# Small SBUF buffers moved to the front, every large buffer at a multiple of 2048 bytes, in a two-layer encoder trunk on one core

## What is computed

```python
x = x + 0.5 * swiglu(rms_norm(x, g1), w_gate, w_up, w_down)      # width 2816
h = rms_norm(x, g2)
xr, yr, q, k, v, g_a, g_b = split(h @ w_in)
y_a = (gelu(yr) * rg_lru(conv(xr))) @ w_up_a                     # recurrence, width 1408
y_b = chunked_attention(norm(q), norm(k), v, rel_table) @ w_up_b # 16 heads of 64
x = x + (sigmoid(g_a) * y_a + sigmoid(g_b) * y_b) @ w_out
x = x + 0.5 * swiglu(rms_norm(x, g3), w_gate2, w_up2, w_down2)
```

## Time and profile before

| | |
|---|---|
| median of 3 runs | 2804.24 us (2801.92 to 2804.95) |
| span of the profiled execution | 2802.1 us |
| mean granted clock of TensorE | 0.995 |
| PE busy | 2759.9 us, 98% of the span |
| POOL, ACT, DVE busy | 42%, 42%, 30% |
| DMA queue of the weights | 28.8% of 16 engines |

### The profile page before, as it was taken

One profiled execution on the slowest core, in us unless ns is written; L12 is line 12 of the kernel. 1 busy time (PEld: TensorE's weight loads), 2 busy tenths in 40 slices (PEclk: granted clock), 3 DMA queues, 4 the chain that ended last, 5 costly groups with the idle time before them and its releaser, 6 DMA issues.

```text
span 2802.1 us, 35532 instructions
## 1 busy us (share of the span) xinstructions
PE 2759.9 (98%) x11968; PEld 2198.7 (78%) x11968; DVE 831.6 (30%) x1515; ACT 1187.7 (42%) x1680; POOL 1179.1 (42%) x524
## 2 busy tenths in 40 slices
PE   8999999999999999999999999999999999999998
PEld 6888878878776688888888888788787757888887
DVE  4222035630015432221142211448100164322222
ACT  5443235742445534443244432457324463444422
POOL 3444444444442234444444444344453422444444
PEclk9999999999999999999999999999999999999999
DMA  7323223332331223232233223232333212223222
GB/s 257 98 92 99 94 84 96 91 100 82 98 98 40 71 91 101 94 99 95 93 99 97 90 94 98 82 94 83 109 94 98 72 41 89 91 90 105 94 91 87
DMA packets 247056, 263.82 MB, mean 94 GB/s; under 512 B 9040, under 2 KB 233072, under 8 KB 246928
## 3 DMA queue, kind: packets, MB, share of 16 engines
q1 hardware_dynamic: 242768, 253.70, 28.8%
q10 hardware_dynamic: 4160, 8.47, 0.9%
HBM read 259.95 MB, written 10.57 MB: 97 GB/s over the span
## 4 chain that ended last, share of the span: by engine, by line
issue 41%; PE 39%; POOL 18%; DVE 1%; POOLq 1%; DMA 0%; ACT 0%; SPq 0%; DVEq 0%; ACTq 0%
POOL wlo L406 18%; PE ps L1087 10%; PE ps L1092 10%; PE ps L1091 10%; PE ps L1287 2%; PE ps L1215 2%; PE ps L1269 1%; PE ps L1200 1%; PE ps L1236 1%; PE ps L1235 1%; PE ps L1231 1%; POOLq L413 0%; DMA x_tok<-in_x 0%; POOLq L405 0%; PE ps L1317 0%
## 5 line engine op out<-in xcount | busy, mean ns | idle before, releaser
L406 POOL TENSOR_TENSOR wlo<-raw,whi 128x1024 fp32r<-128x1024 f32 x475 | 1140.7, 2408 | 1487.6 <-ACT whi L455 1487.2
L1087 PE MATMUL ps<-h_lo,whi 128*128 128x512 f32 x2400 | 946.5, 394 | 21.5 <-DVE h_lo L740 9.8
L1091 PE MATMUL ps<-h_hi,whi 128*128 128x512 f32 x2400 | 937.5, 391 | 0.0
L1092 PE MATMUL ps<-h_hi,wlo 128*128 128x512 f32 x2400 | 937.4, 391 | 0.0
L455 ACT ACTIVATE whi<-raw 128x1024 fp32r<-128x1024 f32 x475 | 499.8, 1055 | 759.0 <-PE ps L1087 696.4
L1087 PEld LDWEIGHTS ps<-h_lo,whi 128*128 128x128 f32 x2400 | 452.5, 189 | 126.9 <-DVE h_lo L740 14.9
L1091 PEld LDWEIGHTS ps<-h_hi,whi 128*128 128x128 f32 x2400 | 452.9, 189 | 97.2 <-issue 3.8
L1092 PEld LDWEIGHTS ps<-h_hi,wlo 128*128 128x128 f32 x2400 | 452.7, 189 | 94.2
L1087 PE MATMUL ps<-act_lo,whi 128*128 128x512 f32 x704 | 278.5, 396 | 0.0
L1091 PE MATMUL ps<-act_hi,whi 128*128 128x512 f32 x704 | 278.5, 396 | 0.0
L1092 PE MATMUL ps<-act_hi,wlo 128*128 128x512 f32 x704 | 278.4, 396 | 0.0
(11 more groups left out here) (139 smaller groups left out, 2643.0 us busy)
## 6 DMA issues: line engine op xcount, KB each, us to landing
raw<-in_w_in SPq DMA_DIRECT2D x124, 512.0 KB, 3.6
raw<-in_w_gate SPq DMA_DIRECT2D x88, 512.0 KB, 3.5
raw<-in_w_up SPq DMA_DIRECT2D x88, 512.0 KB, 3.6
raw<-in_w_down SPq DMA_DIRECT2D x80, 512.0 KB, 3.4
raw<-in_w_up_b SPq DMA_DIRECT2D x19, 512.0 KB, 3.6
rel_band<-rel_rows ACTq DMA_DIRECT2D x1, 8192.0 KB, 38.1
raw<-in_w_out SPq DMA_DIRECT2D x16, 512.0 KB, 3.3
raw<-in_rg_band SPq DMA_DIRECT2D x14, 512.0 KB, 3.5
```

The lines of the kernel that those rows point to most:

```text
L406: nc.gpsimd.tensor_tensor(wlo[:, s, :], raw[:, s, :], whi[:, s, :].bitcast(F32), ALU.subtract).then_inc(lo_made, 1)
L1087: ins = pe.matmul(ps[:, b, :], w_hi, x_lo, start=start, stop=False)
L1091: pe.matmul(ps[:, b, :], w_hi, x_hi, start=False, stop=False)
L1092: return pe.matmul(ps[:, b, :], w_lo, x_hi, start=False, stop=stop)
```

## The change

The small tensors are declared first, padded in front by `line_up` to a multiple of 512 bytes, and behind by `line_up_wide` so that `x` and all large tensors behind it start at a multiple of 2048. Two pads become smaller so that all fits, and `v012` starts at a multiple of 512. No instruction is added, removed or moved; only the addresses in them differ. The table above has the addresses after, beside those before.

```diff
+LINE = 512
+SMALL_END = 200
...
-        x = sb("x", [P, KD, S])
-        h_hi, h_lo = sb("h_hi", [P, KD, S], F32R), sb("h_lo", [P, KD, S], F32R)
-        raw = sb("raw", [P, SLOTS, CW])
-        whi, wlo = sb("whi", [P, SLOTS, CW], F32R), sb("wlo", [P, SLOTS, CW], F32R)
-        tmp = sb("tmp", [P, 2, S])
-
-        square = sb("square", [P, 2, S])
-        rstd = square[:, 0, :]
-        next_gain = sb("next_gain", [P, KD])
+        line_up = sb("line_up", [P, (LINE - (16384 + 4 * 32) % LINE) % LINE // 4])
         ident, ones, ones_head = sb("ident", [P, P]), sb("ones", [P, P]), sb("ones_head", [P, P])
         par = sb("par", [P, NPAR])
         decay = sb("decay", [P, 2, KR])
...
         qg = sb("qg", [P, 1])
         carrier = sb("carrier", [1, HEADS * KS])
         mx, total, inv = sb("mx", [P, 2, KS]), sb("total", [P, 2, KS]), sb("inv", [P, 2, KS])
+        next_gain = sb("next_gain", [P, KD])
+        line_up_wide = sb("line_up_wide", [P, SMALL_END])
+
+        x = sb("x", [P, KD, S])
+        h_hi, h_lo = sb("h_hi", [P, KD, S], F32R), sb("h_lo", [P, KD, S], F32R)
+        raw = sb("raw", [P, SLOTS, CW])
+        whi, wlo = sb("whi", [P, SLOTS, CW], F32R), sb("wlo", [P, SLOTS, CW], F32R)
+        tmp = sb("tmp", [P, 2, S])
+
+        square = sb("square", [P, 2, S])
+        rstd = square[:, 0, :]
...
-                                        ("gate", [P, 2, S], F32), ("pad_f", [P, 2048], F32))
+                                        ("gate", [P, 2, S], F32), ("pad_f", [P, 2048 - 8], F32))
...
-            ("k", [P, KD, S], F32), ("p1", [P, TRI], F32), ("pad_g", [P, R - KD * S - TRI], F32),
+            ("k", [P, KD, S], F32), ("p1", [P, TRI], F32), ("pad_g", [P, R - KD * S - TRI - 128], F32),
             ("v012", [P, 3, D], F32))
```

More of the change, by code:

```diff
@@ L173, in sem @@
             return ctx.enter_context(nc.semaphore(name))
+        line_up = sb("line_up", [P, (LINE - (16384 + 4 * 32) % LINE) % LINE // 4])
+        ident, ones, ones_head = sb("ident", [P, P]), sb("ones", [P, P]), sb("ones_head", [P, P])
+        par = sb("par", [P, NPAR])
+        decay = sb("decay", [P, 2, KR])
+        soft = sb("soft", [P, 4, KR])
+        qg = sb("qg", [P, 1])
+        carrier = sb("carrier", [1, HEADS * KS])
+        mx, total, inv = sb("mx", [P, 2, KS]), sb("total", [P, 2, KS]), sb("inv", [P, 2, KS])
+        next_gain = sb("next_gain", [P, KD])
+        line_up_wide = sb("line_up_wide", [P, SMALL_END])
         x = sb("x", [P, KD, S])
```

## The result

Four runs of each kernel gave 2780.7 us (2779.71 to 2781.43) after and 2804.5 us (2801.92 to 2804.95) before: a ratio of 0.9917, with a 95% interval of 0.9903 to 0.9931. The change takes off 23.8 us, 0.8%. The forecast was 2782.5 us, 21.7 us less than before.

A forecast was written before the change was run, and what follows sets the result against it. PE was taken as the bound, by matmul count times start spacing. 3396 slow matmuls gaining 6.4 ns take 21.7 us off the 2802.1 us span, giving 2780.4; the runs' median lies 2.1 higher, so 2782.5 us, range 2710 to 2808.

The forecast's parts named there:

- What bounds the kernel: PE, busy 98% of the span: the time is the number of matmuls times the spacing of their starts.
- The two kinds and their sizes: Float32r matmuls: 7584 spaced 227.1 ns, streaming `h` or weights; 3396 spaced 233.5 ns, streaming `act`, `u`, `ya` or `m`.
- the reason given: Streaming tiles starting at 32 mod 64 are slow; those on a 64- or 128-byte boundary are fast.
- Part (1): `act`, `u`, `ya`, `m` move from 864 to 0 mod 2048 and become as fast as `h`: 21.7 us less.
- Part (2): `h` and the streaming weights move from 128 to 0 mod 2048, already on the boundary: no gain.
- Part (3): Stationary weights move from 128 to 0; their 189 ns loads lie beside a 227 ns matmul, so shortening would not show.
- Parts (4) to (7): Plain float32 matmuls, POOL/ACT/DVE work, DMA of `raw`, and small buffers: no gain, waits under 1 us in all.
- The second: Rival: the boundary is 256 bytes or more, so `h` speeds up too; 2634 us at full size, likelier 2712; chance 0.18.
- The third: Rival: the address is not the cause of the slow spacing, so nothing changes; 2804 us; chance 0.20.
- The fourth: Rival: equal remainders collide, so the slow spacing spreads to all matmuls; 49 us more, 2853 us; chance 0.12.
- The 16-byte cachelines: Quoted SBUF rule penalizing a crossing to a new cacheline; by it alone nothing would change, 2804 us.
- The 216 ns: Quoted back-to-back matmul gap; if addresses alone kept float32r matmuls from it, the time would fall to about 2658 us.

The follow-up runs named there:

- e5_weights32: The changed kernel with `whi` and `wlo` alone at 32 mod 64, all streaming tiles at 0 mod 64; 2848.2 us.
- e12_swapped: The kernel before with `whi` and `wlo` alone moved to remainder 96 mod 256, that of `act`, `u`, `ya` and `m`, while `h` keeps 128; 2825.8 us.
- e4_overlay32: The changed kernel with a 32-byte pad ahead of the overlaid tensors alone (`act`, `u`, `ya`, `m` and others at 32 mod 2048); 2804.6 us.
- e2_all32: The changed kernel with every large tensor 32 bytes further, all at 32 mod 2048; 2781.1 us.
- e8_two_banks: The changed kernel with the two PSUM banks of a pair taking turns, matmul by matmul, inside `pair()`; 2782.8 us.
- e6_wlo32: The changed kernel with `wlo` alone at 32 mod 64; 2840.2 us.
- e9_offsets128: The changed kernel with streaming tiles at distances from the weights, alike mod 128: `h` 128 bytes, `act` 64, `u` 32, `ya` 96, `m` 16; 2833.1 us.

## Why the prediction was right, and where its reason was wrong

**What bounds the kernel: right.** If the distances of all 10980 float32r matmuls, each stage at its mean, are taken from a run's time, 284 to 293 us are left in every run, whose times go from 2780.7 to 2848.5. Of this scatter, some 3.5 us are the shorter wait for POOL in the slower runs (e5_weights32, e12_swapped).

**The two kinds and their sizes: right.** 7584 fast and 3396 slow matmuls, with a difference read as 6.4 ns from whole windows and 6.67 by all starts. This undersizing is worth 1 us of the 2 by which 21.7 missed 23.8.

**The step that failed: "The weight loads of both take 188 to 189 ns, with the same stationary buffers, so the streaming side makes the difference", and with it "Nothing else that I see separates them".** The stationary buffers were the same, but the pair was not: `h` at 128 met weights at 128, and `act` at 864, which is 96 mod 256, met the same 128. The table of addresses had both facts. A difference between two tiles against a common partner can lie in the tiles or in the match with the partner, and the trace of before could not tell them apart. e4_overlay32 against e2_all32 (same tiles, other weights) and e12_swapped (other weights alone) do. That the change puts streams and weights at the same remainder is why it works; that this remainder is 0 is of no account. So the number held by luck: the change met the true condition along with the one that was named. By the reason given, e5_weights32, with every streaming tile but those of `v` on a multiple of 64, should have run in 2783 us, and it took 2848.2. The prediction's last sentence allows for a reason "that does not move with the addresses"; the true one moves with them, but with the weights' as well.

**Part (1), 6.4 ns x 3396: right in size, by another mechanism. Part (2), `h` gains nothing: right**, since `h` was already like the weights. **Part (3), "whether they shorten or not does not show": wrong in kind.** The load's record stays at 187 to 189 ns, but where the weights lie is half of the cause; 32 bytes on them alone cost 67 us against the changed kernel (e5_weights32). **Parts (4) to (7): right.** Plain float32 matmuls, DVE, ACT and POOL have the same means after, to 1 ns, in the groups of the earlier trace rows. A chunk still lands in 3.4 us; the weights' queue took 30.6% after, 28.8% before and 30.4% in e4_overlay32, which is as slow as the kernel before, so no time follows from it.

**The rivals.** The second, a wider boundary that would speed up `h`: the rule is indeed one of 256 bytes, but of a match, which `h` had. The 13.4 ns above 213.3 (half of the 427 ns at half clock in the earlier trace rows) stayed in the mean of every stage of every arrangement tried, e8_two_banks too; its cause is open. The third had its best witness in the earlier trace rows, `h` running slowly for some steps behind a plain float32 matmul. This is another thing than the slow stages: over the whole trace these steps go unevenly from 224 to 236 ns and end after some eight, while the down products of the kernel before stay between 230 and 236. The change leaves them as they were: in the changed kernel nine steps from 743.29 to 745.36 us are 230 ns each on the mean. The fourth, equal remainders that collide, is the reverse of what was found.

**The rules quoted.** The 16-byte cachelines of the Trainium skill ("SBUF — State Buffer", Specifications) gave "nothing changes", and missed it: 864 and 128 are both multiples of 16. The 216 ns of the Trainium skill for 512 columns ("TensorE: Matmul & The Clock Gate", Back-to-back issue gap), which the page calls the gap of a matmul by itself and not of a stream with weight loads, is met by no float32r stage here; the best stays at 226.7 ns.

**What stays open.** How the two addresses come to matter together, and why the price of a stage varies from 2.2 to 11.1 ns, was not settled. That the load of the next weights and the streaming of the present tile disturb each other in SBUF fits e5_weights32, the swapped roles in `v` and the largest distance in e6_wlo32, but it is only argued: no run took the loads away.

## What to carry to other kernels

In every arrangement tried here the fast stages were those in which the match held. Give the streaming and the stationary operands of float32r matmuls starts that are alike mod 256 bytes; the common remainder made no difference, so one pad at the right place is enough, and a small buffer declared in the wrong place can cost 0.8% here and 2.4% where it splits all pairs. Check it by the distance of successive matmul starts in each stage, not by the share of busy time, which was 98% in both kernels. When a group is slow against a common partner, test the partner's side too before naming the group's own property.

## What the runs showed of the hardware that I had not expected

- Streams and weights alike mod 256: 226.7 ns a matmul of 512 columns. Unlike: 228.9 to 237.8 ns, 233.3 in the plain cases (32 bytes apart). 128 bytes apart gave 232.6, or 232.3 to 232.4 in the overlay. The dearest arrangement, 237.8, had the high part 68 bytes beyond the weights and the low part 124 short of them.
- The weight load's record (187 to 189 ns) does not show it; only the matmuls' spacing does.
- One of the two weight buffers off by 32 bytes cost as much in the `h` stages as both (233.3 ns on the mean in e6_wlo32 and in e5_weights32), while `act`, 64 off in both parts, cost 2.2 ns (e9_offsets128).
- Plain float32 matmuls of 512 columns have records of 592 ns before and 591 or 592 after, although `k` and `square` were unlike before. Their starts, with `k` streaming, lie 429.0 ns apart before and 429.5 after; with `square` streaming against `ones_head` 431.3 and 428.3, which is 0.1 us over the 32 distances and was not looked into.
